# Rotary half exchange by on-chip transfers instead of a TensorE matmul, and weight squares summed in bf16, in a two-layer diffusion block

## The reference

```python
def apply_rope(x, cos, sin):
    ...
    x1, x2 = x[..., :half], x[..., half:]
    return jnp.concatenate([x1 * cos - x2 * sin, x2 * cos + x1 * sin], axis=-1)
```

## Time and profile before

| what | value |
|---|---|
| median of 3 runs | 1800.26 us (1796.07 to 1803.64) |
| the profiled execution | 1800.2 us, its span 1798.4 us |
| mean granted TensorE clock | 0.982 |
| PE busy | 1684.0 us (94% of the span) |
| DVE, POOL, ACT busy | 970.4, 787.5, 662.0 us |

### The profile page before, as it was taken

The page is one execution under the profiler, slowest core; times in us unless marked ns, Lnnn a source line. Parts: engine busy times, 40 slices in busy tenths (PEclk is TensorE's granted clock), DMA queues, the critical chain, the costliest instruction groups (busy, mean ns, idle before and its releaser), DMA issues. The chain is left out here.

```text
span 1798.4 us, 27888 instructions
## 1 busy us (share of the span) xinstructions
PE 1684.0 (94%) x11035; PEld 1241.0 (69%) x11035; DVE 970.4 (54%) x1715; ACT 662.0 (37%) x1218; POOL 787.5 (44%) x575
## 2 busy tenths in 40 slices
PE   7999988977989999999999999997987999999998
PEld 3688877866856678666876687786876645745646
DVE  3544488895458841686428844456995612122112
ACT  3222267775233410233013113225875354053130
POOL 2244435662424563344413343542233657458363
PEclk9999999999989999999999999999999999999999
DMA  9344353322124423245226422443103324334332
GB/s 316 47 107 114 98 139 86 91 59 71 47 71 141 120 82 103 83 131 162 72 70 188 137 62 57 114 101 107 19 2 82 83 71 117 94 90 109 83 82 82
DMA packets 314351, 174.99 MB, mean 97 GB/s; under 512 B 87518, under 2 KB 309614, under 8 KB 314222
## 3 DMA queue, kind: packets, MB, share of 16 engines
q1 hardware_dynamic: 284686, 143.70, 30.3%
q10 hardware_dynamic: 29536, 29.51, 5.1%
HBM read 159.04 MB, written 2.83 MB: 90 GB/s over the span
## 5 line engine op out<-in xcount | busy, mean ns | idle before, releaser
L889 PE MATMUL acc<-act,pair_w 128*128 128x512 f16 x3168 | 582.9, 345 | 7.2 <-ACT act L1283 4.2
L889 PEld LDWEIGHTS acc<-act,pair_w 128*128 128x128 f16 x3168 | 308.8, 99 | 268.2 <-DVE act L1607 10.0
L889 PE MATMUL acc<-act,split_w 128*128 128x512 f32 (+1 forms) x1920 | 381.0, 357 | 8.8 <-DVE act L1871 2.8
L889 PEld LDWEIGHTS acc<-act,split_w 128*128 128x128 f32 x1920 | 308.9, 191 | 62.2 <-DVE act L1871 4.5
L889 PE MATMUL acc<-hidden,split_w 128*128 128x512 f32 (+1 forms) x1584 | 309.2, 357 | 6.6 <-POOL split_w L655 3.6
L652 POOL TENSOR_SCALAR split_w<-raw_w 128x1024 fp32r<-128x1024 f32 (+1 forms) x120 | 126.6, 1055 | 427.6 <-PE acc L889 333.5
L889 PEld LDWEIGHTS acc<-hidden,split_w 128*128 128x128 f32 x1584 | 260.0, 188 | 53.0 <-POOL split_w L655 5.3
L655 POOL TENSOR_TENSOR split_w<-raw_w,split_w 128x1024 fp32r<-128x1024 f32 (+1 forms) x120 | 280.3, 2336 | 10.0
L758 POOL TENSOR_SCALAR pair_raw<-pair_raw,weight_scale 128x1024 f32<-128x1024 f32 x88 | 106.2, 1207 | 357.5 <-ACT pair_w L1457 357.5
L1934 DVE SCALAR_TENSOR_TENSOR mod_acc<-mod_chunk,silu_c,mod_acc 128x256 f32<-128x256 f32 x280 | 223.7, 842 | 4.0
L1632 DVE SCALAR_TENSOR_TENSOR x_t<-acc,mod,x_t 128x512 f32<-128x512 f32 x96 | 60.4, 659 | 257.1 <-PE acc L889 256.6
(11 more groups left out here) (189 smaller groups left out, 1883.3 us busy)
## 6 DMA issues: line engine op xcount, KB each, us to landing
mod_chunk<-in_w_mod ACTq DMA_DIRECT2D x28, 1024.0 KB, 5.2
pair_raw<-in_w_gate SPq DMA_DIRECT2D x44, 512.0 KB, 4.1
pair_raw<-in_w_up SPq DMA_DIRECT2D x44, 512.0 KB, 5.5
raw_w<-in_w_in SPq DMA_DIRECT2D x64, 256.0 KB, 3.7
raw_w<-in_w_down SPq DMA_DIRECT2D x32, 512.0 KB, 4.2
raw_w<-in_w_mod SPq DMA_DIRECT2D x24, 512.0 KB, 4.2
mod_start<-in_w_mod SPq DMA_DIRECT2D x8, 1024.0 KB, 11.7
ks<-q_split SPq DMA_DIRECT2D x64, 96.0 KB, 2.2
```

The lines of the kernel that those rows point to most:

```text
L889: mm = pe.matmul(acc[slot][:, a:b], weights[:, part == 2, k, :], moving[:, part == 1, k, a:b], start=(k == 0 and part == 0), stop=(k == n ...
```

## The change

First, `after_norm` is gone from PE. In its place ACT has `swap_halves(j - 3)`, between `take_root(j - 1)` and the copy of unit j: it waits for `q_n` (and for the last rotation to be done with `q_sin`), and issues four transfers of 32 partitions by 512 fp32 values (64 KB each) from `q_n` into `q_sin`, each 32-partition block to its partner's place. DVE's `rotate` waits for all four, and multiplies `q_sin` in SBUF where it read PSUM before. The constant `swap` and its load are gone.

Second, `sum_weights` multiplies with a bf16 `ones16`, and reads only the upper 16 bits of each fp32 sum as bf16 values. So each sum is of values cut to bf16.

```diff
+            pool.memset(ones16[:, :], 1.0).then_inc(filled, 1)
...
+                if n == 0:
+                    pe.wait_ge(filled, 3)
                 if f == 0:
                     pe.wait_ge(act_scaled, 5 * l + 1)
-                pe.matmul(mod_ps[:, 0:2], ones[:, :], weight_sum[:, 2 * f:2 * f + 2], start=True, stop=True).then_inc(weight_ps, 1)
+                high = weight_sum[:, 2 * f:2 * f + 2].bitcast(BF16)[:, 1:4:2]
+                pe.matmul(mod_ps[:, 0:2], ones16[:, :], high, start=True, stop=True).then_inc(weight_ps, 1)
...
-                def after_norm(j):
-                    if not 0 <= j < 16 or QKV[j][0] not in "qk":
-                        return
-                    i = l * N_ROPE + rope_before(j)
-                    pe.wait_ge(q_normed, l * N_QK + qk_before(j) + 1)
-                    if i >= 1:
-                        pe.wait_ge(q_sin_ready, i)
-                    pe.matmul(small[:, 0:LAT], swap[:, :], q_n[i % 2][:, :], start=True, stop=True).then_inc(q_swapped, 1)
...
-                    after_norm(j - 3)
                     after_copy(j - 1)
...
+                def swap_halves(j):
+                    if not 0 <= j < 16 or QKV[j][0] not in "qk":
+                        return
+                    r = l * N_ROPE + rope_before(j)
+                    sc.wait_ge(q_normed, l * N_QK + qk_before(j) + 1)
+                    if r:
+                        sc.wait_ge(q_ready, r)
+                    for p in range(0, P, 32):
+                        sc.dma_start(q_sin[p:p + 32, :], q_n[r % 2][p ^ 32:(p ^ 32) + 32, :]).then_inc(swap_in, 16)
...
                 for j in range(16):
                     take_root(j - 1)
+                    swap_halves(j - 3)
...
-                    ve.wait_ge(q_swapped, r + 1)
-                    if r:
-                        ve.wait_ge(q_ready, r)
-                    ve.tensor_tensor(q_sin[:, :], small[:, 0:LAT], sin[:, :], ALU.mult).then_inc(q_sin_ready, 1)
+                    ve.wait_ge(swap_in, 64 * (r + 1))
+                    ve.tensor_tensor(q_sin[:, :], q_sin[:, :], sin[:, :], ALU.mult).then_inc(q_sin_ready, 1)
```

More of the change, by code:

```diff
@@ L206, in trunk @@
 def trunk(nc, x, c, ctx, c_ctx, w_mod, b_mod, norm_attn, norm_ffn, w_in, qk_norm, sink, rpb, w_out,
-          w_gate, w_up, w_down, k_ident, k_pairs, k_swap, k_cos, k_sin, k_window, k_columns, out):
+          w_gate, w_up, w_down, k_ident, k_pairs, k_cos, k_sin, k_window, k_columns, out):
     inv_dram = nc.dram_tensor("inv_rows", [2, 2, TOK], F32, kind="Internal").ap()
@@ L230, in trunk @@
         pair_ones = place("pair_ones", [P, P], F32)
-        swap = place("swap", [P, P], F32)
         ones = place("ones", [P, P], F32)
+        ones16 = place("ones16", [P, P], BF16)
         cos = place("cos", [P, LAT], F32)
@@ L362, in trunk @@
         qkv_copied, q_sq, q_ssq, q_root, q_inv = sem("qkv_copied"), sem("q_sq"), sem("q_ssq"), sem("q_root"), sem("q_inv")
-        q_normed, q_swapped, q_cos_ready, q_sin_ready, q_ready = (
-            sem("q_normed"), sem("q_swapped"), sem("q_cos_ready"), sem("q_sin_ready"), sem("q_ready"))
+        q_normed, swap_in, q_cos_ready, q_sin_ready, q_ready = (
+            sem("q_normed"), sem("swap_in"), sem("q_cos_ready"), sem("q_sin_ready"), sem("q_ready"))
         v_ps, v_ready, v_hi = sem("v_ps"), sem("v_ready"), sem("v_hi")
@@ L470, in _ @@
             load_start(2)
-            for dst, src in ((pair_ones, k_pairs), (swap, k_swap), (cos, k_cos), (sin, k_sin)):
+            for dst, src in ((pair_ones, k_pairs), (cos, k_cos), (sin, k_sin)):
                 sp.dma_start(dst[:, :], src[:, :]).then_inc(consts_in, 16)
@@ L1971 @@
 N_VECS = 4 + 3 * DEPTH
-N_CONST = 7
+N_CONST = 6
 def shape_constants():
@@ L1980, in shape_constants @@
     pairs = (p[:, None] // 64 == p[None, :] // 64).astype(f)
-    swap = (p[:, None] == (p[None, :] ^ 32)).astype(f)
     t = np.arange(LAT)
@@ L1995, in shape_constants @@
         columns[:, VARIANT[cb]] = np.where(ok, 0, NEG)
-    return {"k_ident": ident, "k_pairs": pairs, "k_swap": swap, "k_cos": cos, "k_sin": sin.astype(f),
+    return {"k_ident": ident, "k_pairs": pairs, "k_cos": cos, "k_sin": sin.astype(f),
             "k_window": window, "k_columns": columns}
```

## The result

The changed kernel takes 1818.5 us (median of 4 runs, 1815.5 to 1821.6) where the kernel before took 1799.4 (4 runs beside it): a ratio of 1.0101, 95% interval 1.0075 to 1.0127. It is slower by 1%, outside the predicted range of 1786 to 1815. The profiled execution took 1816.5 us, its span is 1814.7 and its mean granted clock 0.976 (0.982 before).

The account below looks back on a forecast made before the run. PE was taken as the bound in the input projections. From 1800.2 us, 16.4 came off for the exchange, 16.9 was added for stalls and 3.5 came off for the weight sums: 1797.2, no change that can be told, range 1786 to 1815.

Parts of the forecast that it names:

- Term 1: Exchange steps and two waits for `q_n` leave PE in the input projections, with lost clock regained: 16.4 us less.
- Term 2: Transfers replacing the exchange make DVE's reciprocal late, so PE stalls in the input projections: 16.9 us more.
- The chain: Issue, landing, rotation and reciprocal, counted from S, the start of PE's next product: reciprocal ready at S + 5.80.
- the ten named: Places where a rotation and a reciprocal meet: m = 5, 6, 8, 10 and 11 in each layer.
- 10 x 1.55 + 1.4: Stall sum: 1.55 us at each of ten places, 1.4 more at m = 8 of layer 1; 16.9 us.
- the first transfer can be issued where the copy stood: On ACT, the first of four transfers is issued 0.35 us after PE's next product starts.
- Slower: the transfers wait among SP's: Rival: transfers share engines with SP's; issue 0.60 and landing 3.5 us give 1814.2 us; chance 0.22.
- The clock rival: Each stall drops PE to its lower clock for 3.3 us, costing 1.6 us a place: 1813 us; chance 0.08.
- I would be wrong in kind if DVE's later work lets PE wait for something else, the copy or the split weights.: Sign in the profile after: PE waiting for other late DVE work than the reciprocal; no size given.
- Term 3: 44 bf16 weight sums on PE take 0.06 us instead of 0.14, all of it counting: 3.5 us less.
- The held-up product: Rival: DVE's rotation product, line 1737, meets a POOL instruction, losing up to 2.1 us a place: 1818 us; chance 0.04.
- Hidden anyway: Rival: issues overlap or landing is quick, so the reciprocal is ready when PE needs it: 1780.3 us; chance 0.08.

## Why the prediction was wrong

**Term 1, what leaves PE (16.4 us): right.** Without new waits layer 0's projection is 6.6 us shorter (8 x 0.86 = 6.9) and layer 1's 10.6 (6.9 + 1.0 + 1.6 = 9.5): 17.2 us.

**Term 2, the stalls: mechanism right, usual size near, the sum too small.** The chain had the reciprocal ready at S + 5.80; at the usual place it was ready at S + 6.01, since four issues took 2.45 us, 0.61 each and not 0.50. The places are the ten named. The step that failed is "10 x 1.55 + 1.4": one place's price was taken for all. By the waits in the brackets four places cost 15.2 us, where 7.6 were charged, so the total is 24.6 and not 16.9; by the distances from S it is 26.2. At m = 8 of layer 1 it was the step "the first transfer can be issued where the copy stood": the issue waited 1.1 us longer, for `q_n`, and the rotation then took 0.74 more beside POOL. At the other three the transfers were slow. From the first issue to the rotation a usual place has 3.9 us; the first of layer 0 has 6.2 (issues 2.98, the last landing 3.8), the first of layer 1 5.5 (issues 3.44), m = 10 of layer 1 5.8 (issues 2.92, the last landing 3.6). The earlier trace rows had a warning for m = 8 only: the units for which PE had waited for `q_n` were those without slack.

**"Slower: the transfers wait among SP's" was given 0.22 as a price for every place.** Its mark, issue and landing above 4.8 us together, was passed at three places of ten, worth 5.7 us. SP had issues of its own in flight at these three, at the first only towards the end. But beside three of SP's issues (m = 8 of layer 1) and beside five (the unit at 126.27 us) the four took 2.48 us, so that SP's transfers are the cause is not shown.

**The clock rival was given 0.08 and only for every place.** The four long waits are the case that the earlier trace rows didn't cover. Behind the usual waits of 1.6 us the windows show a clock of 1.00, behind three of the four long ones 0.50 or 0.51 (behind the one of 3.40 it stayed at 1.00). That is 5.3 us, in no term of the sum.

**"I would be wrong in kind if DVE's later work lets PE wait for something else, the copy or the split weights."** That happened, for the value tiles. It is a small part in the changed kernel (0.81 and 0.22 us for `take_values`), and became the main loss as soon as the reciprocal had been moved. The prediction dismissed m = 7 and 12 since a value unit has no reciprocal; it has value tiles, in the same place behind the rotation.

**Term 3, the sums (-3.5): the price near, its place in the sum wrong.** A sum gives back 0.11 us at its place, where 0.08 was taken, and the stage of layer 1 1.5 us. "These sums stand between products of a PE without gaps" is false in layer 0, and the earlier trace rows showed the gap of 2.9 us. In layer 0 the sums moved PE, POOL and DVE against each other: DVE's block took 2.4 us longer beside POOL, the wait for it grew to 5.35 us, and the clock fell. In the profiled execution the two stages together lost 2.3 us where 3.5 were to be gained.

**The account**, against the forecast of 1797.2 in one execution of 1816.5: stalls by their distances +9.3 (26.2 for 16.9), clock behind them +5.3, value tiles +1.0, term 1 -0.8, sums +5.8. That is 20.6 of 19.3. Two differences belong to no term: the start of the kernel, up to the first sum of squares, was 5.1 us shorter in this profile, and the stretch from layer 1's first score product to its first pair product 3.2 us longer; such differences stand between other pairs of profiles too. With these two it comes to 18.7, and that it closes so well is partly luck.

**The held-up product (0.04)** happened, though not as a rule: line 1740 took up to 2.46 us and 18.9 us in 16, where 16 x 0.69 is 11.1. At m = 8 of layer 1 it is 0.74 of the 4.83, and the one of 2.36 us ahead of `q_n` lost 1.7 us, which is more than the 1.1 that the issue came late. Whether the work between them would have moved with it no run shows. **Hidden anyway (0.08)** was right in one sense: the transfers can be hidden whole, but by DVE's order and not by quick landing.

Not tried: `take_values` first in the kernel before (its trace has no wait of PE for them in the projections), transfers issued by another queue, and fewer, larger transfers.

## What to carry to other kernels

When work moves from the bound engine to a slower path that has slack on average, look for what stands in order behind its consumer: here two things for PE's next product, neither of which needed the transfer, stood behind the rotation. Moving them ahead turned 1% slower into 1% faster, and moving only the one that the waits named gave 22 of the 35 us.

Price each place of a repeated stall by itself, first of all the place where the old profile already had a wait. And before a gain on the bound engine is counted, find its next wait for another engine. A gain ahead of it is worth nothing unless the work that is waited for ends earlier too; here that work ended later, at its new place against POOL, and the longer wait cost clock as well.

## What the runs showed of the hardware

- Four transfers of 64 KB from ACT's queue took 2.45 us to issue at a usual place, 0.61 each, up to 1.43 for one and up to 3.44 for four. The earlier trace rows had 0.60 at the median for the stacking copies on SP's queue: that was the near row, and 0.50 was chosen below it without need.
- A gap of 2.87 us at one place of the same work was followed by the lower clock in one profile of five, one of 5.35 us in six of six. Behind the gaps of 1.5 to 1.6 us at the transposes it never was, but behind one of 1.83 us it was (reciprocal first, layer 0), and behind PE's wait of 0.85 or 0.86 us for `q_n` in layer 1 it was in two profiles of five with the exchange on PE. So the length of one gap did not decide it.
- DVE's block of late modulation took very different times for the same work, as it fell against POOL's. One product of line 1937 took 0.47 us at least, 0.49 at the median and 2.58 at most of 280 in the changed kernel; those above 0.49 all ran beside an instruction of POOL. Fourteen products behind tile 7 of the feed-forward, in the kernel before and in the one with the sums only:

```profile
654.03 8.31 DVE L1934 SCALAR_TENSOR_TENSOR mod_acc<-mod_chunk,silu_c,mod_acc 128x256 f32<-128x256 f32 x14
```

```profile
652.16 13.98 DVE L1939 SCALAR_TENSOR_TENSOR mod_acc<-mod_chunk,silu_c,mod_acc 128x256 f32<-128x256 f32 x14
```

The second began 1.9 us earlier. That its place against POOL alone makes the difference is read from the timelines, not shown by a run that changes POOL's place.
